# Expert weights applied at the copy out of PSUM, an accumulating scatter, and routing and first block reordered

## The chip, the cores and the metric

One NeuronCore of a Trainium2 chip runs the whole kernel. The metric is the device time of the execution in microseconds (us), as the median of the runs. The engines are PE (TensorE, matmul), DVE (VectorE), ACT (ScalarE), POOL (GpSimd) and SP (SyncE, which here only issues DMAs).

## The reference

One layer of a decoder trunk over 1024 prompt tokens and 32 sample tokens (TOK = 1056 rows of D = 1024, all float32). Attention, a recurrent branch and projections give x1; the change touches what follows:

```python
h2 = rms_norm(x1) * (1 + scale) + shift
g_logits = h2 @ w_rg + b_rg                    # 4 groups; g_star = argmax, p_group = softmax
in_group = (h2 @ w_re + b_re)[group g_star]    # 8 experts of the group
top_v, top_i = top_k(in_group, 2)
gate_w = softmax(top_v) * p_group[g_star]      # two weights per token
# the 2112 (token, expert) pairs, sorted by expert, in blocks of 128 rows of one expert
for each block: yb = (silu(x @ w_gate[e]) * (x @ w_up[e])) @ w_down[e]   # 1024 -> 512 -> 1024
moe[token] += yb * gate_w                      # two rows are added for each token
y = x1 + gate * rms_norm(moe)
```

There are 32 experts with 6.3 MB of weights each, and every expert's weights are read for at least one block. With these inputs there are 34 blocks.

## The kernel before

Tokens lie in nine tiles of 128 rows (the last has 32), in three groups of three tiles. The last group's mix (output projection) steps `mix(last, q)`, q from 0 to 7, are followed by norms, transposes and router logits of its three tiles; meanwhile DVE runs `best` (top group, top two experts) for the six earlier tiles. When the last logits are kept, DVE makes the one-hot of all 18 (tile, choice) pairs (`oh`, and `ohs`, their sum), PE ranks the pairs within their experts by 54 small matmuls with triangular and full ones (`ubf`, semaphore rt_pe 1), DVE turns ranks into slots (block, row) and one-hots of them, PE multiplies these with token numbers (18 matmuls, rt_pe 2), and DVE writes `slot_to` (destination row in y_dram: token, plus a plane offset for the second choice) and `slot_from` (token). GpSimd then gathers rows of h2 by an indirect DMA into `xg`. Softmax weights stay in `wts`, by token.

Every float32 matrix goes through PE as the sum of a rounded part and a rest: ACT rounds (`wg_up`, `wu_up`, `wd_up`, `x_up`, `a_up`), DVE subtracts (`wg_low` and so on), and PE does three products (up times up, up times low, low times up). A block n in steady state has on PE: transposes of the next block's x (L2282), up products of n (24 matmuls of 512 columns), first half of the gate products of n + 1, transposes of act_h (L2314), second half of the gate products of n + 1, and down products of n in two halves of the columns (y_half, y_done). ACT has x_up of n + 1, wd_up, one half of wu_up, a_up, the other half, the sigmoid, wg_up of n + 2 in two halves, and the two copies of y out of PSUM into `ysb[s]` (L1268, L1270). DVE has the matching subtractions and act_h (L1846), which stands behind both halves of wd_low. Each engine's instructions run in the order in which they are written. SP loads the weights of a block in the order gate, up, down, each when its buffer (two per matrix) is free. POOL's order in the loop is: gather of n + 3 (copy of the indices, indirect DMA), then scatter of n into y_dram (copy of the indices, indirect DMA). ACT's copy into `ysb[s]` waits for the scatter of n - 2 alone, by a semaphore for each of the two buffers. y_dram holds two planes, one row for each (token, choice), and no row is written twice.

The tail, when all scatters have landed: SP loads for each tile both planes' rows (`fy[:, t, 0:2, :]`, 1 MB), ACT multiplies the first by its weight (L1288), DVE adds the second times its weight (L1876), ACT squares and sums (L1296) and takes the root (L1298), DVE does the reciprocal, scales (L1888) and adds x1 (L1893), SP stores the tile. DVE's `add_second` of tile t + 1 stands ahead of the reciprocal of tile t.

## Time and profile before

| | us |
|---|---|
| median of 3 runs (1862.25 to 1864.72) | 1863.24 |
| the profiled execution | 1863.41 |
| its span | 1861.3 |

| engine | busy us | share |
|---|---|---|
| PE | 1707.8 | 92% |
| DVE | 1269.3 | 68% |
| ACT | 1053.0 | 57% |
| POOL | 269.4 | 14% |

The span is cut by the profile into 40 slices of 46.5 us. Attention and the recurrent branch run to about 600 us, the branch projections and the mix to about 1120, the last norms and the routing to about 1165, the expert blocks to about 1811 and the tail to 1861. DMAs moved 416.60 MB, 224 GB/s on the mean, but about 370 GB/s all through the expert blocks; 392.71 MB of them went on SP's queue and 17.73 MB on GpSimd's. A weight matrix of 2 MB lands 8 to 14 us after its issue there. The page's DMA line (busy tenths by slice) has 4 to 8 in the first six slices, 1 in the next seven, about 6 where the projections begin, and 8 to 9 in the expert blocks. The chain of the page has PE for 25% of the span, DMAs for 6%, DVE for 5%.

### The profile page before, as it was taken

The numbers are of one execution on the slowest core, as the hardware profiler recorded it, in microseconds if no ns is written. First come the engines' busy times: TensorE is split into PE (matmuls) and PEld (weight loads), VectorE is DVE, ScalarE is ACT, GpSimd is POOL, SyncE is SP. The second block draws the span as 40 slices with busy tenths as digits, with TensorE's granted clock in tenths as the row PEclk, the third lists the DMA queues.
The fourth block names the chain that finished last, engine by engine and source line by source line (L and its number), as shares of the span: only waits on it lengthen the run. The fifth ranks groups of instructions, "written<-read, shape, count | busy, mean of one in ns | idle before, by whom it ended". The sixth has DMA issues, their size and how long they took to land. (4 is left out here: it accounts for less than half of the span.)

```text
span 1861.3 us, 26670 instructions
## 1 busy us (share of the span) xinstructions
PE 1707.8 (92%) x10120; PEld 1473.3 (79%) x10120; DVE 1269.3 (68%) x1647; ACT 1053.0 (57%) x1465; POOL 269.4 (14%) x302
## 2 busy tenths in 40 slices
PE   6999889999999899999999994799999999999980
PEld 3889658888888899999999973587887888887860
DVE  4524367888887644545454667698988889998957
ACT  4535245555666533435344533578787877777745
POOL 0000011111110000000000200133333333242310
PEclk9999899999999899999999995899999999999995
DMA  8554441111111663734474663699999998998957
GB/s 346 185 184 142 159 163 48 55 52 49 50 49 57 247 203 124 260 124 152 159 258 151 205 227 124 251 386 373 384 373 375 363 378 351 367 373 348 378 198 279
DMA packets 101298, 416.60 MB, mean 224 GB/s; under 512 B 16039, under 2 KB 43847, under 8 KB 87496
## 3 DMA queue, kind: packets, MB, share of 16 engines
q1 hardware_dynamic: 85488, 392.71, 56.4%
q0 software_dynamic: 10704, 17.73, 2.6%
q10 hardware_dynamic: 5016, 4.93, 0.8%
q8 instruction: 61, 1.00, 0.2%
q14 instruction: 29, 0.24, 0.0%
HBM read 384.06 MB, written 51.13 MB: 234 GB/s over the span
## 5 line engine op out<-in xcount | busy, mean ns | idle before, releaser
L1076 ACT ACTIVATE wup<-wraw 128x1024 fp32r<-128x1024 f32 x120 | 126.7, 1059 | 274.7 <-PE ps L1898 238.8
L1564 DVE TENSOR_TENSOR wlow<-wraw,wup 128x1024 fp32r<-128x1024 f32 x120 | 146.8, 1224 | 166.2 <-ACT wup L1076 165.9
L1705 DVE TENSOR_TENSOR wg_low<-wg,wg_up 128x2048 fp32r<-128x2048 f32 x68 | 152.9, 2289 | 38.1 <-ACT wg_up L1190 38.1
L1705 DVE TENSOR_TENSOR wu_low<-wu,wu_up 128x2048 fp32r<-128x2048 f32 x68 | 155.6, 2289 | 16.9 <-ACT wu_up L1196 16.1
L1705 DVE TENSOR_TENSOR wd_low<-wd,wd_up 128x2048 fp32r<-128x2048 f32 x68 | 152.7, 2288 | 14.9 <-ACT wd_up L1243 14.8
L1190 ACT ACTIVATE wg_up<-wg 128x2048 fp32r<-128x2048 f32 x68 | 126.7, 1909 | 38.8 <-DMA wg<-w_gate 37.4
L1196 ACT ACTIVATE wu_up<-wu 128x2048 fp32r<-128x2048 f32 x68 | 130.1, 1914 | 25.0 <-PE ps L1898 25.0
L1026 ACT ACTIVATE pp<-ps,ngm 128x256 f32<-128x256 f32 x128 | 59.5, 470 | 136.4 <-DVE skd L1449 120.7
L1898 PE MATMUL ps<-h_up,wup 128*128 128x384 f32 (+1 forms) x384 | 128.1, 333 | 8.1 <-ACT yl L1148 4.2
L1898 PE MATMUL ps<-h_up,wlow 128*128 128x384 f32 (+1 forms) x384 | 126.7, 330 | 0.0
L1898 PE MATMUL ps<-h_low,wup 128*128 128x384 f32 (+1 forms) x384 | 126.6, 330 | 0.0
L1243 ACT ACTIVATE wd_up<-wd 128x2048 fp32r<-128x2048 f32 x68 | 126.3, 1911 | 0.0
L1898 PE MATMUL ps<-wg_up,x_up 128*128 128x512 f32 x272 | 112.2, 413 | 4.5 <-DVE x_low L1827 4.5
L1898 PE MATMUL ps<-wu_up,x_up 128*128 128x512 f32 x272 | 110.6, 407 | 0.0
L1898 PE MATMUL ps<-wd_up,a_up 128*128 128x512 f32 x272 | 108.7, 400 | 1.4 <-DVE a_low L1850 1.4
L1898 PE MATMUL ps<-hp_up,wA_up 128*128 128x352 f32 x312 | 108.2, 347 | 0.7 <-DVE hp_low L1327 0.7
L1898 PE MATMUL ps<-wg_low,x_up 128*128 128x512 f32 x272 | 108.1, 398 | 0.0
L1898 PE MATMUL ps<-hp_up,wB_up 128*128 128x352 f32 x312 | 106.4, 341 | 1.6 <-ACT gB L1001 1.6
L1898 PE MATMUL ps<-wg_up,x_low 128*128 128x512 f32 x272 | 107.8, 396 | 0.0
L1898 PE MATMUL ps<-wd_low,a_up 128*128 128x512 f32 x272 | 107.6, 396 | 0.0
L1898 PE MATMUL ps<-wd_up,a_low 128*128 128x512 f32 x272 | 106.8, 393 | 0.0
L1898 PE MATMUL ps<-wu_low,x_up 128*128 128x512 f32 x272 | 106.8, 393 | 0.0
(366 smaller groups left out, 4660.8 us busy)
## 6 DMA issues: line engine op xcount, KB each, us to landing
wg<-w_gate SPq DMA_DIRECT2D x34, 2048.0 KB, 12.6
wu<-w_up SPq DMA_DIRECT2D x34, 2048.0 KB, 13.5
wd<-w_down SPq DMA_DIRECT2D x34, 2048.0 KB, 8.2
wraw<-w_ga SPq DMA_DIRECT2D x24, 512.0 KB, 3.6
wraw<-w_gr SPq DMA_DIRECT2D x24, 512.0 KB, 3.6
wraw<-w_at SPq DMA_DIRECT2D x24, 512.0 KB, 3.5
wraw<-w_lr SPq DMA_DIRECT2D x24, 512.0 KB, 3.4
wraw<-w_out SPq DMA_DIRECT2D x24, 512.0 KB, 3.7
```

Of the source, the lines that this page charges most:

```text
L1026: act.activation(pp[:, s % 2, a, :], ps[:, 3 + s % 2, a * 2 * P:(a + 1) * 2 * P], ACT.Exp, bias=ngm[:, s % 2, a:a + 1], scale=SCALE, accum ...
L1076: act.activation(wup[n % UP][:, :, :], wraw[n % RAW][:, :, :], ACT.Copy).then_inc(w_rounded, 1)
L1190: act.activation(halves_of(wg_up)[h], halves_of(wg[s])[h], ACT.Copy).then_inc(g_rounded, 1)
L1196: act.activation(halves_of(wu_up)[h], halves_of(wu[s])[h], ACT.Copy).then_inc(u_rounded, 1)
L1243: act.activation(halves_of(wd_up)[h], halves_of(wd[s])[h], ACT.Copy).then_inc(d_rounded, 1)
L1564: V.tensor_tensor(wlow[n % RAW][:, :, :], wraw[n % RAW][:, :, :], wup[n % UP][:, :, :].bitcast(F32), ALU.subtract).then_inc(w_split, 1)
L1705: V.tensor_tensor(low[:, k0:k1, :], whole[:, k0:k1, :], up[:, k0:k1, :].bitcast(F32), ALU.subtract).then_inc(done, 1)
L1898: return pe.matmul(out, lhsT, rhs, start=start, stop=stop, skip_group_check=True)
```

## The change

1. Weights. After `wts`, DVE splits the weights into three bf16 parts (`wpart`) and multiplies the slots' block one-hot by them (`rhs3`); PE sends them to their slots by 18 matmuls of 144 columns (rt_pe 3), DVE adds the three parts into `wsl` (weight by slot and block). POOL copies a block's column into `wcur[:, s]` (`slot_weight`), and ACT's two copies out of PSUM take it as their scale, behind a wait on w_ready.
2. Scatter. y_dram has one row per token. SP writes zeros into it during the attention (nine DMAs). The scatter adds to the rows (`compute_op=ALU.add`) with the indices `slot_row`. POOL waits for each scatter's landing before it goes on; `st_y` is now one semaphore, and ACT's copy into `ysb[s]` waits for `32 * i`: all scatters of the pairs of blocks before its own.
3. Tail. One row per token is loaded (0.5 MB per tile), `weigh` and `add_second` are gone, the table for the root is loaded ahead of the first tile, and the addition of x1 goes to POOL for odd tiles.
4. Routing. `choose` makes the one-hots, for tiles 0 to 5 at q = 4 and for 6 to 8 at the end; PE's `rank` of tiles 0 to 5 goes behind the mix, the rest behind the last one-hot. PE's transposes of the last group wait for their own tile, with other banks. The last group's `best` is one tile and then two, and the second half of the first wg_low goes between them.
5. First block (`begin`). x_up/x_low of block 1 goes between the halves of its gate split, the subtractions wd_low of block 0 go behind act_h and a_low, and both halves of wu_up behind a_up.
6. Last block. The down weights of the last block are rounded into a buffer of their own (`wd_last`, in the gate buffer's place) already in the block before.

```diff
@@ -633,6 +641,12 @@
...
+                if i == 2:
+                    for t in range(TILES):
+                        n = P if t < BLKS else 2 * NS + 1
+                        sp.dma_start(y_dram[t * P:t * P + n, :].rearrange("p (a n) -> p a n", a=D // KV),
+                                     vtok[0:n, 0:1, :].broadcast_to([n, D // KV, KV])).then_inc(st_zero, 16)
+            sp.wait_ge(st_zero, 16 * TILES)
...
-                pool.tensor_copy(idx[:, 2 + s:3 + s], slot_to[:, bass.ds(n, 1)]).then_inc(idx_ready, 1)
+                pool.tensor_copy(idx[:, 2 + s:3 + s], slot_row[:, bass.ds(n, 1)]).then_inc(idx_ready, 1)
...
-                                        bounds_check=SPARE[1], oob_is_err=False).then_inc(st_y[s], 16)
+                                        bounds_check=TOK + NS, oob_is_err=False, compute_op=ALU.add).then_inc(st_y, 16)
+
+            def slot_weight(n, s):
+
+                pool.tensor_copy(wcur[:, s:s + 1], wsl[:, bass.ds(n, 1)]).then_inc(w_ready, 1)
...
@@ -845,14 +864,25 @@
...
+            pool.wait_ge(tables, 4)
+            for s in range(2):
+                pool.tensor_copy(wcur[:, s:s + 1], wsl[:, s:s + 1]).then_inc(w_ready, 1)
+            pool.wait_ge(st_zero, 16 * TILES)
...
                 for s in range(2):
...
+                    slot_weight(2 * i + s + 2, s)
+                    pool.wait_ge(st_y, 32 * i + 16 * s + 16)
             for s in range(2):
...
+                pool.wait_ge(st_y, 32 * more + 16 * s + 16)
...
+            pool.wait_ge(ld_x1, 32)
+            for t in range(1, TILES, 2):
+                pool.wait_ge(f_norm, t + 1)
+                pool.tensor_tensor(fy[:, t, :], fy[:, t, :], x1f[:, t, :], ALU.add).then_inc(y_added_p, 1)
...
         def _(act):
...
+            def act_block(i, s, ahead=2, begin=False):
...
+                if ahead >= 1 and not begin:
+                    round_x(n + 1, 1 - s)
                 if ahead >= 1:
-                    round_x(n + 1, 1 - s)
-                round_down(0, n, s, i + 1)
-                round_down(1, n, s, i + 1)
-                if ahead >= 1:
-                    round_up(0, n + 1, 1 - s, i + 1 + s)
+                    round_down(0, n, s, i + 1)
+                    round_down(1, n, s, i + 1)
+                    if not begin:
+                        round_up(0, n + 1, 1 - s, i + 1 + s)
...
+                if begin:
+                    round_up(0, 1, 1, 1)
                 if ahead >= 1:
...
@@ -1263,18 +1300,23 @@
                 if ahead >= 2:
...
+                if ahead == 1:
+                    round_last(0)
+                    round_last(1)
...
-                ge(act, st_y[s], 16 * i)
-                act.activation(ysb[:, s, 0:512], ps[:, 4, :], ACT.Copy)
+                ge(act, st_y, 32 * i)
+                act.wait_ge(w_ready, n + 1)
+                act.activation(ysb[:, s, 0:512], ps[:, 4, :], ACT.Copy, scale=wcur[:, s:s + 1])
...
-                act.activation(ysb[:, s, 512:1024], ps[:, 5, :], ACT.Copy).then_inc(y_kept, 1)
+                act.activation(ysb[:, s, 512:1024], ps[:, 5, :], ACT.Copy, scale=wcur[:, s:s + 1]).then_inc(y_kept, 1)
...
+            round_x(1, 1)
...
-            for s in range(2):
-                act_block(0, s)
+            act_block(0, 0, 2, True)
+            act_block(0, 1)
...
                 for s in range(2):
...
@@ -1282,18 +1324,11 @@
...
-            def weigh(t):
+            act.activation(fst[:, 0, 1:2], eps[:, :], ACT.Sqrt)
...
                 for t in range(t0, t1):
...
+            def choose(t0, t1):
+
+                ts, n = slice(t0, t1), t1 - t0
+                k(V.tensor_copy(eix[:, ts, :], ei8[:, ts, 0:2]))
+                k(V.scalar_tensor_tensor(eix[:, ts, :], bc(gix[:, ts].unsqueeze(2), (P, n, 2)), float(EPG), eix[:, ts, :], ALU.mult, ALU.add))
+                k(V.tensor_tensor(oh[:, ts, :, :].rearrange("p t k e -> p (t k) e"), bc(iot[:, 0:NE].unsqueeze(1), (P, 2 * n, NE)),
+                                  bc(eix[:, ts, :].rearrange("p t k -> p (t k)").unsqueeze(2), (P, 2 * n, NE)), ALU.is_equal))
+                V.tensor_tensor(ohs[:, ts, :], oh[:, ts, 0, :], oh[:, ts, 1, :], ALU.add).then_inc(rt_ready, 1)
+
             def split_half(h, whole, up, low, rounded, done, n):
...
@@ -1719,10 +1763,12 @@
...
                 if q == 4:
+                    choose(0, 3 * last)
+                if q == 4:
...
-                if q >= KC - 3:
-                    split_gate(q - KC + 3, 0, 0)
+                if q == KC - 3:
+                    split_gate(0, 0, 0)
...
             def last_half(j):
...
@@ -1754,19 +1800,16 @@
...
-            for j in range(2):
-                keep_logits(last, j, ((6, 1)[j], 0))
-            dve.wait_ge(lg_kept, 3 * last + 2)
-            best(3 * last, 3 * last + 2)
-            keep_logits(last, 2, (2, 0))
+            keep_logits(last, 0, (6, 0))
+            dve.wait_ge(lg_kept, 3 * last + 1)
+            best(3 * last, 3 * last + 1)
+            split_gate(1, 0, 0)
+            for j in (1, 2):
+                keep_logits(last, j, ((1, 2)[j - 1], 0))
...
-            best(TILES - 1, TILES)
-            k(V.tensor_copy(eix[:, :, :], ei8[:, :, 0:2]))
-            k(V.scalar_tensor_tensor(eix[:, :, :], bc(gix[:, :].unsqueeze(2), (P, TILES, 2)), float(EPG), eix[:, :, :], ALU.mult, ALU.add))
-            k(V.tensor_tensor(oh[:, :, :, :].rearrange("p t k e -> p (t k) e"), bc(iot[:, 0:NE].unsqueeze(1), (P, TK, NE)),
...
+            whole = wts[:, :, :].rearrange("p t k -> p (t k)")
+            k(V.tensor_copy(wpart[0][:, :], whole))
+            k(V.tensor_tensor(wrest[0][:, :], whole, wpart[0][:, :], ALU.subtract))
+            k(V.tensor_copy(wpart[1][:, :], wrest[0][:, :]))
+            k(V.tensor_tensor(wrest[1][:, :], wrest[0][:, :], wpart[1][:, :], ALU.subtract))
+            k(V.tensor_copy(wpart[2][:, :], wrest[1][:, :]))
+            for a in range(3):
+                ins = V.tensor_tensor(rhs3[:, :, a, :], ohblk[:, :, :], bc(wpart[a][:, :].unsqueeze(2), (P, TK, MAXB)), ALU.mult)
+            ins.then_inc(rt_ready, 1)
+            k(V.tensor_scalar(over[:, :], slot_to[:, :], 12, None, ALU.logical_shift_right))
+            k(V.scalar_tensor_tensor(slot_row[:, :], over[:, :], float(TOK), slot_from[:, 0:MAXB], ALU.mult, ALU.add))
...
-                if ahead >= 1:
+                if ahead >= 1 and not begin:
...
-                split_down(0, n, s)
-                split_down(1, n, s)
+                if ahead >= 1 and not begin:
+                    split_down(0, n, s)
+                    split_down(1, n, s)
...
-                if ahead >= 1:
+                if begin:
+                    split_down(0, 0, 0)
+                elif ahead >= 1:
...
+                if begin:
+                    split_down(1, 0, 0)
+                    split_up(0, 1, 1)
                 if ahead >= 1:
...
                 if ahead >= 2:
...
+                if ahead == 1:
+                    for h in range(2):
+                        split_half(h, wd[1], wd_last, wd_low[1], d_rounded, d_split, n + 1)
...
+            dve.wait_ge(rt_pe, 3)
+            k(V.tensor_copy(wsl[:, :], ps[:, 7, 0:MAXB]))
+            for a in (1, 2):
+                ins = k(V.tensor_tensor(wsl[:, :], wsl[:, :], ps[:, 7, a * MAXB:(a + 1) * MAXB], ALU.add))
+            dve.sem_inc(tables, 1)
...
+            split_x(1, 1)
...
-            with dve.Fori(0, more) as i:
+            dve_block(0, 0, 2, True)
+            dve_block(0, 1)
+            with dve.Fori(1, more) as i:
                 for s in range(2):
...
+
+            def rows(t):
+                return P if t < BLKS else NS
+
+            def rank(t0, t1):
+
+                for t in range(t0, t1):
+                    out = ps[:, 7, t * NE:(t + 1) * NE]
+                    for b in range(min(t + 1, TILES)):
+                        w = ubf[0:rows(b), 0 if b == t else 1, :]
+                        ins = mm(out, w, ohs[0:rows(b), b, :], b == 0, b == min(t, TILES - 1))
+                return ins
+
             for q in range(KC):
...
+            pe.wait_ge(rt_ready, 1)
+            rank(0, 3 * last)
...
-            pe.wait_ge(mix_kept, 6 * last + 6)
-            pe.wait_ge(mix_sq, 6 * last + 6)
             for j in range(3):
+                pe.wait_ge(mix_kept, 6 * last + 3 + j)
+                pe.wait_ge(mix_sq, 6 * last + 3 + j)
                 if j == 2:
...
-                turn(last, j, 0, (7, 4, 7)[j])
-                turn(last, j, 1, (3, 5, 3)[j])
+                turn(last, j, 0, (4, 0, 4)[j])
+                turn(last, j, 1, (5, 3, 5)[j])
+                if j:
+                    pe.wait_ge(mix_kept, 6 * last + 4 + j)
+                    pe.wait_ge(mix_sq, 6 * last + 4 + j)
...
-            pe.wait_ge(rt_ready, 1)
-
-            def rows(t):
-                return P if t < BLKS else NS
-
-            for t in range(TILES + 1):
-                out = ps[:, 7, t * NE:(t + 1) * NE]
-                for b in range(min(t + 1, TILES)):
-                    w = ubf[0:rows(b), 0 if b == t else 1, :]
-                    ins = mm(out, w, ohs[0:rows(b), b, :], b == 0, b == min(t, TILES - 1))
-            ins.then_inc(rt_pe, 1)
-
-            pe.wait_ge(rt_ready, 3)
+            pe.wait_ge(rt_ready, 2)
+
+            rank(3 * last, TILES + 1).then_inc(rt_pe, 1)
+
+            pe.wait_ge(rt_ready, 4)
             for q in range(TK):
...
+                down = wd_last if last else wd_up
                 for nn, done in enumerate((y_half, y_done)):
...
                     for m in range(FC):
                         if nn == 0 and m % 2 == 0:
...
-                        for a, w in ((a_up, wd_up), (a_up, wd_low[s]), (a_low, wd_up)):
-                            ins = mm(ps[:, 4 + nn, :], a[:, m, :], w[:, m, cols], m == 0 and a is a_up and w is wd_up, m == FC - 1 and a is a_low)
+                        for a, w in ((a_up, down), (a_up, wd_low[s]), (a_low, down)):
+                            ins = mm(ps[:, 4 + nn, :], a[:, m, :], w[:, m, cols], m == 0 and a is a_up and w is down, m == FC - 1 and a is a_low)
...
+            pe.wait_ge(rt_ready, 5)
+            for q in range(TK):
+                n = rows(q // 2)
+                ins = mm(ps[:, 7, 0:3 * MAXB], ohslot[0:n, q, :], rhs3[0:n, q, :, :].rearrange("p a b -> p (a b)"), q == 0, q == TK - 1)
+            ins.then_inc(rt_pe, 1)
...
```

## Rows read from the trace of the kernel before

**Rows 1.** busy us of PE, PEld, DVE, ACT, POOL; clock, DMA share, GB/s

```profile
1196.00:1500.00 304.00, 299.33 (x1381) 244.65 (x1380) 268.75 (x165) 233.84 (x181) 96.26 (x64) 1.00 0.90 365
```

**Rows 2.** the chain that ended last: start us, us, what

```profile
1223.65 0.89 PE ps L2282 x8
...
1537.62 0.89 PE ps L2282 x8
...
1555.66 0.89 PE ps L2282 x8
...
1811.86 3.15 DMA y_dram<-ysb,idx
```

**Rows 3.** waits in the expert blocks: who, for whom, us in total, times, longest

```profile
ACT wg_up L1190 <- DMA wg<-w_gate: 33.5, 26, 4.0
```

**Rows 4.** timeline of DVE, the tail's end: start us, us, engine, line, what

```profile
1851.28 1.23 DVE L1893 TENSOR_TENSOR fy<-fy,x1f 128x1024 f32<-128x1024 f32 x1
1852.43 1.27 DVE L1876 SCALAR_TENSOR_TENSOR fy<-fy,wts 32x1024 f32<-32x1024 f32 x1
...
1855.12 1.22 DVE L1893 TENSOR_TENSOR fy<-fy,x1f 128x1024 f32<-128x1024 f32 x1
...
1857.75 1.21 DVE L1893 TENSOR_TENSOR fy<-fy,x1f 32x1024 f32<-32x1024 f32 x1
```

**Rows 5.** timeline of ACT, the tail

```profile
1820.28 1.15 ACT L1288 ACTIVATE fy<-fy,wts 128x1024 f32<-128x1024 f32 x1 [9.63 <-DMA fy<-y_dram]
...
1830.64 1.06 ACT L1296 ACTIVATE fjunk<-fy 128x1024 bf16<-128x1024 f32 x1 [0.56 <-DVE fy L1876]
```

**Rows 6.** the tile qst: instructions, duration ns min/median/max, first and last start

```profile
L807 POOL COPY qst<-oT x128: 283/287/1238, 229.9 to 580.9; 64x128 f32<-64x128 f32 x128
```

**Rows 7.** timeline of POOL in the attention

```profile
459.00 2.51 POOL L807 COPY qst<-oT 64x128 f32<-64x128 f32 x2 [2.26 <-ACT oT L1055]
```

**Rows 8.** timeline of DVE at the same time

```profile
458.80 1.26 DVE L1512 SCALAR_TENSOR_TENSOR gC<-gC,yl 128x1056 f32<-128x1056 f32 x1 [3.25 <-ACT gC L1018]
460.10 1.26 DVE L1513 SCALAR_TENSOR_TENSOR olst<-gC,olst 128x1056 f32<-128x1056 f32 x1
```

**Rows 9.** the tensor y_dram, 1196 to 1793 us: its scatters' landings

```profile
DMA to landing us min/median/max: 5.2/11.1/12.0
```

**Rows 10.** the tile xg, 1196 to 1793 us: its gathers' landings

```profile
DMA to landing us min/median/max: 11.2/13.2/15.3
```

**Rows 11.** timeline of POOL: two of the scatters

```profile
1227.05 1.01 POOL L839 DMA_INDIRECT y_dram<-ysb,idx  x1 [0.90 <-POOL idx L836]
...
1778.12 1.03 POOL L839 DMA_INDIRECT y_dram<-ysb,idx  x1 [0.88 <-POOL idx L836]
```

**Rows 12.** timeline of ACT: the copies out of PSUM behind these

```profile
1241.92 0.58 ACT L1268 ACTIVATE ysb<-ps 128x512 f32<-128x512 f32 x1
...
1790.19 0.60 ACT L1268 ACTIVATE ysb<-ps 128x512 f32<-128x512 f32 x1 [2.26 <-PE ps L1898]
```

**Rows 13.** timeline of PE, last group and ranks

```profile
1126.87 1.94 PE L2203 MATMUL ps<-ident,xh 128*128 128x128 f32 x8 [7.40 <-DVE x L1730]
...
1146.52 1.95 PE L1898 MATMUL ps<-ohs,ubf 128*128 128x32 bf16 x54 [4.80 <-DVE ohs L1769]
```

**Rows 14.** the page's costliest groups: busy us, mean ns, idle before

```profile
L1705 DVE TENSOR_TENSOR wd_low<-wd,wd_up 128x2048 fp32r<-128x2048 f32 x68 | 152.7, 2288 | 14.9 <-ACT wd_up L1243 14.8
```

**Rows 15.** timeline of DVE, routing and first block

```profile
1158.83 2.03 DVE L1802 TENSOR_TENSOR rhs<-ohblk,tpid 128x864 bf16<-128x864 bf16 x2
...
1172.98 1.23 DVE L1827 TENSOR_TENSOR x_low<-ps,x_up 128x1024 fp32r<-128x1024 f32 x1 [1.05 <-ACT x_up L1238]
...
1194.26 0.68 DVE L1846 TENSOR_TENSOR act_h<-sgm,ps 128x512 f32<-128x512 f32 x1
```

**Rows 16.** timeline of the last block (PE's last up product, DVE)

```profile
1798.00 0.40 PE L1898 MATMUL ps<-wu_up,x_low 128*128 128x512 f32 x1
...
1799.73 0.68 DVE L1846 TENSOR_TENSOR act_h<-sgm,ps 128x512 f32<-128x512 f32 x1
```

More of the change, by code:

```diff
@@ L312, in build @@
         x1f = at("x1f", [P, TILES, D], ew0)
-        fy = at("fy", [P, TILES, 2, D], e0)
+        fy = at("fy", [P, TILES, D], e0)
+        wd_last = at("wd_last", [P, FC, D], e0, F32R)
         fjunk = at("fjunk", [P, D], ew0 + EW, BF16)
@@ L357, in build @@
         cmpb = rtm("cmpb", [P, MAXB - NE, NE])
+        rhs3 = rtm("rhs3", [P, TK, 3, MAXB], BF16)
+        wpart = [rtm(f"wpart{i}", [P, TK], BF16) for i in range(3)]
+        wrest = [rtm(f"wrest{i}", [P, TK]) for i in range(2)]
+        over = rtm("over", [P, MAXB], I32)
         iot = at("iot", [P, P], 3 * big - 2 * P)
@@ L367, in build @@
         mod_dram = nc.dram_tensor("mod_dram", [2, 4, AM, 512], F32)
-        y_dram = nc.dram_tensor("y_dram", [SPARE[1] + 1, D], F32)
+        y_dram = nc.dram_tensor("y_dram", [TOK + NS + 1, D], F32)
         def sem(name):
@@ L759, in _ @@
             sp.dma_start(x1f[0:NS, BLKS, :], x1_dram[SEQ:TOK, :]).then_inc(ld_x1, 16)
-            for s in range(2):
-                sp.wait_ge(st_y[s], 16 * more + 16)
-                sp.sem_inc(idx_seen, 1)
+            sp.wait_ge(st_y, 32 * more + 32)
+            sp.sem_inc(idx_seen, 1)
             for t in range(TILES):
@@ L1243, in round_down, with round_last @@
                 act.activation(halves_of(wd_up)[h], halves_of(wd[s])[h], ACT.Copy).then_inc(d_rounded, 1)
+            def round_last(h):
+                act.wait_ge(ld_d[1], 16 * more + 16)
+                act.activation(halves_of(wd_last)[h], halves_of(wd[1])[h], ACT.Copy).then_inc(d_rounded, 1)
             def gate_sigmoid(n):
@@ L1274, in _ @@
             round_gate(0, 1, 1, 1)
+            round_x(1, 1)
             round_gate(1, 1, 1, 1)
-            for s in range(2):
-                act_block(0, s)
+            act_block(0, 0, 2, True)
+            act_block(0, 1)
             with act.Fori(1, more) as i:
@@ L1282, in _ @@
             act_block(more, 1, 0)
-            def weigh(t):
+            act.activation(fst[:, 0, 1:2], eps[:, :], ACT.Sqrt)
+            for t in range(TILES):
                 n = P if t < BLKS else NS
                 act.wait_ge(ld_rows[t % LF], 16 * (t // LF + 2))
-                act.activation(fy[0:n, t, 0, :], fy[0:n, t, 0, :], ACT.Copy, scale=wts[0:n, t, 0:1]).then_inc(f_first, 1)
-            weigh(0)
-            for t in range(TILES):
-                n = P if t < BLKS else NS
-                if t + 1 < TILES:
-                    weigh(t + 1)
-                act.wait_ge(f_sum, t + 1)
-                act.activation(fjunk[0:n, :], fy[0:n, t, 0, :], ACT.Square, accum_out=fst[0:n, t, 0:1]).then_inc(ch_fin, 1)
+                act.activation(fjunk[0:n, :], fy[0:n, t, :], ACT.Square, accum_out=fst[0:n, t, 0:1]).then_inc(ch_fin, 1)
                 act.wait_ge(ch_fin, t + 1)
```

51 lines of the change are left out of this document (23 added, 28 removed).

## The prediction

> **What bounds the kernel now.** I read the page for the stages, then the busy time by stage, the chain of waits, the waits by pair, and the timelines of the three places that the diff touches.
>
> The expert blocks take a third of the span. From 1196 to 1500 us TensorE is busy 299.3 of 304 at a granted clock of 1.00 (2.4 GHz), VectorE 268.8, ScalarE 233.8, and the DMA engines 90% [rows 1]; the stretch on to 1793 is like it. The chain has PE's eight transposes at the head of a block 18.04 us apart [rows 2]: that is the pace, and there are 34 blocks. ScalarE waits for the gate weights in 26 of them, 33.5 us in total [rows 3], nearly all of it hidden behind PE's work. So three resources are within a tenth of each other here: the reader is to see that nothing may be added to the DMA queue or to ScalarE without asking twice. Behind the last block there is no PE work: VectorE repeats a cycle of 3.84 us per tile of the output, nine times, back to back [rows 4]. Ahead of the first block the routing is a serial chain on VectorE with PE and GpSimd taking turns. Tail and routing are pure latency, and what is taken out of them comes off the time in full.
>
> **The tail.** The last scatter lands at 1811.86 + 3.15 = 1815.0 [rows 2]; the span ends at 1861.3, so the tail is 46.3 us. The cycle [rows 4]: addition of x1 1.15 (1851.28 to 1852.43), then 2.69 for the addition of the second expert's row, the reciprocal and the scaling by norm and gain. The change takes out ScalarE's weighting (1.15 [rows 5]) and VectorE's second-row addition (1.27, of which 1.18 counts: instructions overlap by 0.09, as 1.23 and 1.15 show), leaving 2.69 - 1.18 = 1.51, and with the addition of x1 2.66 for the five even tiles; the four odd ones have 1.51, whose addition goes to GpSimd: 5 x 2.66 + 4 x 1.51 = 19.3. In front: the first tile came 5.2 after the landing with 1 MB [rows 5]; with 0.5 MB it is between 2.6 and 5.2, I take 3.9; square and root about 1.5 (1.06 for the square [rows 5], accumulator read and root behind it). The root's table is loaded early, under the load's latency. Behind: from the last addition's end at 1858.96 to the end 2.3 [rows 4]. Sum without GpSimd: 3.9 + 1.5 + 19.3 + 2.3 = 27.0, a gain of 19.3.
>
> GpSimd's additions are the unknown. Two copies of 0.28 each [rows 6] took 2.51 together when they met two VectorE instructions with two SBUF inputs; they ended when the second of those ended, and VectorE's lasted its plain 1.26 [rows 7, 8]. So GpSimd gave way to both, and did not get in between them. An addition of 1024 elements on GpSimd isn't in the trace: below, as on VectorE, 1.2; above, eight such copies for each of two inputs, 4.5; I take 2.3, eight copies. VectorE's reciprocal, one column with nothing read beside it, leaves a gap ahead of each scaling in which GpSimd can begin. If VectorE then waits, four additions cost 9.2, else nothing, for then they run beside it. I take the waiting: the tail is 36.2, gain 10.1, ends 19.3 and 1.3 (four at 4.5).
> The Trainium skill has this as a rule that speaks against the change (SBUF — State Buffer, "Who interferes with whom"): a VectorE instruction with two SBUF inputs contends with a GpSimd instruction that reads SBUF, as an exclusive lock held for a whole instruction. The trace shows the half in which GpSimd waits; by the rule VectorE waits too when GpSimd comes first, by the trace alone that stays open.
>
> **Accumulating scatter.** Its bytes: 2112 rows over 34 blocks, 62 rows of 4 KB, 0.25 MB more to read per block. At 365 GB/s [rows 1] that is 0.7 us of DMA per block in 18.04, a share of 0.90 becoming 0.94. Still under PE; but gate weights that land late already make ScalarE wait, so a few more blocks will slip: I take 3 us over the phase, from 0 to 15. The last scatter, alone on the queues, is on the path: with a read before the write between 0 and another 3.15, I take 1.5.
> New waits: GpSimd now waits for each scatter's landing before the next gather, which is queued behind it. Scatters land 11.1 after issue [rows 9], gathers 13.2 [rows 10]. A scatter is issued 3.4 after the head of the block (1223.65 to 1227.05 [rows 2, 11]), the next gather some 2.5 behind it; now it goes behind the landing: 3.4 + 11.1 + 2.5 + 13.2 = 30.2 into a block, needed two blocks on, at 36.1. Slack 5.9. Each even block's copy of its first half out of PSUM waits for the scatter issued in the same block (before, for the one ahead of it). Issue to copy, in the first of the 16 even blocks behind block 0: 1227.05 to 1241.92, 14.9; in the last: 1778.12 to 1790.19, 12.1 [rows 11, 12]; mean of the 16, 14.1. At 11.1 the wait costs nothing; at 14 it catches only blocks that wait for PE's second half anyway. The scale in the copy and the extra small GpSimd copy are hidden in the same gaps: 0.
> The Trainium skill (Collectives: The Full Stack, "The bandwidth ceiling: the fold count and why AG ≠ RS ≠ AR") has an add in the DMA read two sources, with two descriptors per chunk on one ring, so twice the read traffic. No row here has such a DMA; by that rule the sum would go the way of rival A, below, instead of the forecast's.
>
> **Zeroing y_dram** adds nine DMAs, 4.3 MB, near 362 us behind the y weights on SP's queue, with the gate-matrix load queued behind them. The page's DMA line has one tenth in that slice: the price is 0, and up to 2 if that load comes late.
>
> **Routing.** PE's first transposes of the last group waited for the third tile's half [rows 13]; now they wait for their own tile, and half a weight split (2.29, the size of those in [rows 14]) goes out of VectorE's way: between 0.6 and 2.0 earlier, 1.3. Of 54 rank matmuls in 1.95 [rows 13], 21 go ahead: 0.75. The one-hot of three tiles instead of nine saves 0.5, but two tiles instead of one go through the choice at the end, less than half a microsecond of it lost. Together -2.4 (from 1 to 4).
> Behind that the weights' table is added ahead of the up-weight split on VectorE: five tiny operations of 0.2, three products of 1.02 as the two in [rows 15], two of 0.2: 4.5. The first x_low at 1172.98 had 1.05 of idle ahead of it, so it comes at 1172.98 - 2.4 + 4.5 - 1.05 = 1174.0, 1.1 later than before. The routing gain is spent, and 18 matmuls lie in PE's idle time.
>
> **First block.** act_h (1194.26 [rows 15]) stood behind both wd_low halves, 2 x 2.29 less overlap, 4.4 [rows 14]; now it doesn't: 1.1 - 4.4 = -3.3. But both halves must still be done. VectorE owes 4.4 at the head of the second block and makes up 18.04 - 18.04 x 0.88 = 2.1 in a block, so PE waits some 2.3 there. Net -1.0, from +1 to -4.5 (nothing paid back, and PE's clock up earlier because it idles less).
>
> **Last block.** act_h was at 1799.73, PE's products done by 1798.4 [rows 16]; with wd_last it waits for PE alone: -1.3, with a shorter cold stretch -1.5 (0 to -3). The rounding moves into ScalarE's and VectorE's idle time before 1790.
>
> **Sum**, against the profiled execution's own 1863.41 (span 1861.3; 0.2 over the median of three runs, 1863.24): -1.0 (routing and first block) + 3.0 + 1.5 - 1.5 - 10.1 = -8.1, so 1855.3, and about 1855 by the median.
>
> **Rivals.**
> A, slower: the scatter's landing. Alone on the queues it lands in 3.15 [rows 2], beside the weights in 11.1 [rows 9]: its rows wait for turns among theirs. If the 62 rows of 128 that carry data take a second turn, half of the landing comes on top, 16.5. Then even blocks stall by 16.5 - 14.1 = 2.4 on ScalarE, 16 times, 38 us; where the second half wasn't ready (about a third) it is absorbed: +26, 1881. The gather is then 0.4 from its limit; at a landing of 22 it would be over it too, +110 and more. It decides from a landing of about 15. For it: ScalarE's chain to PE is tight; against: a row's two reads may go as one turn, +2 to 3.
> B, better: GpSimd's additions cost VectorE nothing, and the tail gives 19.3: 1846. For it: VectorE's instructions beside GpSimd's copies were never longer [rows 8]. Against: GpSimd's were tiny.
> C, no change: the DMA share is the true bound of the blocks, the extra read costs half of its 0.7 on each of 33 blocks, +12 instead of +3: 1864. For: the waits of [rows 3]. Against: PE at 98% in [rows 1].
>
> **Numbers.** Forecast 0.40 (own range 1849 to 1861), A 0.24, B 0.23, C 0.13. What this measurement can tell from no change is about 0.2%, 3.7 us. Faster by more: forecast nearly whole and B, 0.61; within: C and the edge, 0.14; slower: A, 0.25. The range that leaves 2 in 10 out: from 1842 (B with the better ends) to 1880 (most of A).
>
> **What would show it.** The landing of the y_dram scatters beside the weights (11 to 14 right, over 15 A); ScalarE's idle time before the first ysb copy in even blocks; turn-to-turn time 18.04 between 1200 and 1790; DMA share up by 0.04; VectorE's gaps in the tail equal to GpSimd's additions (lock) or none (B); x_low within 1.5 of 1174; the tail 36 (27 for B). Wrong if blocks grow by over 0.3 us each, or if the tail gives less than 8.

## The result: 2.1% slower, and the profile after

The changed kernel takes 1902.59 us (median of four runs, 1899.35 to 1904.34), the kernel before 1862.74 beside it: ratio 1.0211, 95% interval 1.0193 to 1.0229. Forecast were 1855 and a range up to 1880. The profiled execution is 1901.59 us, its span 1899.7.

The busy time by stage, in the window of [rows 1] and the one behind it (busy us of PE, PEld, DVE, ACT, POOL; clock, DMA share, GB/s):

```profile
1196.00:1500.00 304.00, 284.35 (x1267) 229.88 (x1266) 254.05 (x154) 218.03 (x169) 76.28 (x73) 0.97 0.89 341
1500.00:1830.00 330.00, 312.57 (x1415) 253.64 (x1414) 276.80 (x168) 241.35 (x185) 90.79 (x85) 0.98 0.85 332
```

In the first of them TensorE, VectorE and ScalarE do 5 to 7% less than in [rows 1], and GB/s falls from 365 to 341: nothing has become busier, all wait for something. TensorE's granted clock falls too, from 1.00 to 0.97; that is taken up below. The waits in the blocks (who, line, for what: us in total, times, longest) say for what:

```profile
POOL idx L841 <- DMA y_dram<-ysb,idx: 402.9, 31, 15.0
...
DVE x_low L1881 <- ACT x_up L1268: 48.4, 30, 3.3
ACT ysb L1309 <- DMA y_dram<-ysb,idx: 47.6, 15, 3.8
...
ACT wg_up L1220 <- DMA wg<-w_gate: 7.8, 14, 1.6
```

GpSimd (L841, the index copy ahead of the gather) spends 403 us waiting for landings, and ScalarE's even-block copy (L1309) is stalled 15 times. The wait for gate weights of [rows 3], 33.5 us, has shrunk to 7.8: weights are early now, because the rest is late. The landings beside the weights (first line the scatters, median 11.1 in [rows 9], second the gathers, median 13.2 in [rows 10]):

```profile
DMA to landing us min/median/max: 12.9/16.1/17.5
...
DMA to landing us min/median/max: 10.2/11.0/12.6
```

The chain of waits, which in [rows 2] ran along PE's transposes 18.04 us apart, runs from scatter to scatter, about 20 us apart, until the tail:

```profile
1327.67 16.02 DMA y_dram<-ysb,idx
1347.08 16.30 DMA y_dram<-ysb,idx
1367.15 15.94 DMA y_dram<-ysb,idx
1387.56 16.52 DMA y_dram<-ysb,idx
...
1855.89 5.71 DMA y_dram<-ysb,idx
1861.69 3.41 DMA fy<-y_dram
```

The next timeline, of GpSimd, ScalarE and VectorE in an even block, shows what hangs on a landing (start, us, engine, line, what, in brackets the idle time ahead and its releaser):

```profile
1347.08 2.74 POOL L854 DMA_INDIRECT y_dram<-ysb,idx  x1 [0.88 <-POOL idx L851]
...
1363.41 0.69 ACT L1309 ACTIVATE ysb<-ps,wcur 128x512 f32<-128x512 f32 x1 [3.51 <-DMA y_dram<-ysb,idx]
1363.96 0.18 POOL L841 COPY idx<-slot_from 128x1 int32 x1 [13.36 <-DMA y_dram<-ysb,idx]
...
1364.57 1.03 ACT L1268 ACTIVATE x_up<-ps 128x1024 fp32r<-128x1024 f32 x1
1365.00 1.05 POOL L844 DMA_INDIRECT xg<-h_dram,idx  x1 [0.86 <-ACT ysb L1311]
1365.63 1.23 DVE L1881 TENSOR_TENSOR x_low<-ps,x_up 128x1024 fp32r<-128x1024 f32 x1 [3.01 <-ACT x_up L1268]
1366.05 0.20 POOL L851 COPY idx<-slot_row 128x1 int32 x1
1367.15 1.59 POOL L854 DMA_INDIRECT y_dram<-ysb,idx  x1 [0.89 <-POOL idx L851]
```

One landing, at 1347.08 + 16.30 = 1363.4, releases two engines. GpSimd needs 3.8 us to the next scatter (0.6 to the copy, copy 0.2, 0.85, gather 1.05, copy 0.2, 0.89), so its loop is landing plus about 4. It waits for ScalarE's copies of y only twice in all the blocks: the loop, and not TensorE, sets when a scatter goes out. ScalarE has stood 3.51 us, its x_up and VectorE's x_low (3.01 idle) with it: TensorE is tied to the same landing.

What TensorE sees of it are pauses ahead of its transposes of act_h. The first line is the wait before the change, the second after it; then one of the pauses, and the clock right behind it (the stretch from 1373 to 1374 us; the clock is the 0.50):

```profile
PE ps L2314 <- DVE act_h L1846: 9.5, 8, 2.1
```

```profile
PE ps L2385 <- DVE act_h L1901: 37.4, 17, 2.6
```

```profile
1372.58 1.13 PE L2385 MATMUL ps<-ident,act_h 128*128 128x128 f32 x4 [2.55 <-DVE act_h L1901]
```

```profile
1373.00:1374.00 1.00, 1.00 (x6) 0.90 (x5) 1.00 (x1) 0.26 (x1) 0.00 (x0) 0.50 0.99 385
```

Before the pause the granted clock is 1.00 (2.4 GHz), behind it 0.50 (1.2 GHz) for some 3 us, with matmuls of 512 columns 0.43 us apart instead of 0.23; the same happens in ten of the 16 even blocks between 1208 and 1808 us. Over these 600 us the clock is 0.97 on the mean where it was 1.00, which takes 17 us of full clock away. By TensorE's account the blocks' 43.9 us below are some 28 of waiting for act_h and some 15 of lower clock. How many of the 43.9 would be left at full clock isn't shown; as GpSimd's loop hardly ever waits for TensorE, the lower clock may cost little of its own.

Where the 38.4 us of span went: to the first scatter +0.1 (1208.1 to 1208.2); from the first to the last scatter 603.8 to 647.7, **+43.9**; last landing 3.15 to 5.71, +2.6; from there to the end 46.3 to 38.1, -8.2. The first-to-last figure is used below for every kernel, from the row that gives its scatters' first and last start.

### The profile page after: what moved, and what is told of

Same layout as the page of the kernel before. It is cut to its first block and busy times, and to the rows that moved or that the text cites. A ratio compares the mean times of both kernels' runs of the same rounds, so it can differ in the third digit from the quotient of the medians.

```text
span 1899.7 us, 26818 instructions
## 1 busy us (share of the span) xinstructions
PE 1726.9 (91%) x10138; PEld 1485.3 (78%) x10138; DVE 1271.0 (67%) x1651; ACT 1048.2 (55%) x1457; POOL 260.4 (14%) x340
## 5 line engine op out<-in xcount | busy, mean ns | idle before, releaser
L1749 DVE TENSOR_TENSOR wg_low<-wg,wg_up 128x2048 fp32r<-128x2048 f32 x68 | 152.9, 2288 | 20.3 <-ACT wg_up L1220 20.1
L1959 PE MATMUL ps<-wg_up,x_up 128*128 128x512 f32 x272 | 119.0, 438 | 4.8 <-DVE x_low L1881 4.6
L1959 PE MATMUL ps<-wg_low,x_up 128*128 128x512 f32 x272 | 113.9, 419 | 0.0
L1959 PE MATMUL ps<-wg_up,x_low 128*128 128x512 f32 x272 | 112.9, 415 | 0.0
L1959 PE MATMUL ps<-wu_up,x_low 128*128 128x512 f32 x272 | 106.4, 391 | 0.0
L1959 PE MATMUL ps<-wd_up,a_up 128*128 128x512 f32 x264 | 104.8, 397 | 0.0
```

Of the source, the lines that this page charges most:

```text
L1749: V.tensor_tensor(low[:, k0:k1, :], whole[:, k0:k1, :], up[:, k0:k1, :].bitcast(F32), ALU.subtract).then_inc(done, 1)
L1959: return pe.matmul(out, lhsT, rhs, start=start, stop=stop, skip_group_check=True)
```

## The experiments

Three things came together in the blocks: the **addition** in the transfer, **GpSimd's wait** for the landing (ahead of the next gather), and **ScalarE's stricter wait** in even blocks. The experiments fill the table of the three. The kernel before, run beside them, had medians of 1860.6 to 1864.2 us, so a difference between two experiments' medians can be off by some us; where it matters, the one by the ratios is given too. "Landing" is from here on the median of all 34 scatters. The first theory was that GpSimd's loop alone did it.

**1. Plain scatter, both waits.**

```diff
-  ..., oob_is_err=False, compute_op=ALU.add).then_inc(st_y, 16)
+  ..., oob_is_err=False).then_inc(st_y, 16)
```

> The changed kernel with a plain scatter in the place of the accumulating one; every wait stays. It leaves out the addition of a token's two experts: the row written later overwrites the other. Theory (GpSimd's own loop: landing plus 4.3 us for the two index copies and two issues, against TensorE's 18.04 us a block): the landing beside the weights goes from 16.0 back to 11-12 us, the loop needs 15.5-16.5 us, TensorE sets the pace again at 18.04 us a block, and of the 47.3 us nearly all come back, with about 2.5 us at the last landing: 1851 to 1857 us. Rival A (ScalarE's wait in the 16 even blocks is what costs): the same direction, but only the 26 us priced on record come back, 1875 to 1880. Rival (the wait itself costs, whatever the landing): 1890 or more.

1865.28 us, 1.0017 of before (1.0000 to 1.0033). Neither number was met: the landing is 14.7, not 11 to 12.

```profile
1318.86 15.25 DMA y_dram<-ysb,idx
1337.90 15.65 DMA y_dram<-ysb,idx
1357.30 15.11 DMA y_dram<-ysb,idx
```

These three land in 15.3 on the mean, where the same plain scatter landed in 11.1: it now goes out right behind its predecessor's landing and a gather. The loop of these rows is 19.2 us, again the landing plus 4, and still above 18.04; over all blocks (616.8 us from the first to the last scatter) it is 18.7. TensorE's waits for act_h are 22.4 us, 13 more than before the change, which is all that the blocks have grown by; its clock stays at 1.00 from 1208 to 1808 us.

**2. ScalarE's wait relaxed, all else as changed.** Two semaphores in the place of one, so that each ysb half waits for its own last scatter.

```diff
-  ge(act, st_y, 32 * i)
+  ge(act, st_y[s], 16 * i)
```

> The changed kernel with ScalarE's wait in the even blocks put back from the scatter of the block before to that of two blocks before; GpSimd keeps its own wait for every landing. Theory (GpSimd's loop sets the pace, ScalarE's wait only shows it): no change, 1898 to 1904 us. Rival A on record (the even blocks' ScalarE wait costs 26 us over 16 blocks): 1874 to 1883.

1866.16 us, 1.0029 (1.0010 to 1.0047): some 35 us back. The theory with its fixed landing falls: GpSimd's wait is still there, and yet the blocks take 615.2. The chain shows how:

```profile
1384.28 10.72 DMA y_dram<-ysb,idx
1403.56 9.48 DMA y_dram<-ysb,idx
1417.93 13.52 DMA y_dram<-ysb,idx
```

The landing is 12.9 instead of 16.0, and it varies from 6.8 to 16.5: it isn't a constant of the transfer. That without ScalarE's tie the scatters drift against the weights' transfers, and some meet them at a better moment, would fit; it isn't shown.

The loop itself is still there. GpSimd goes on from a landing without any other wait in 30 blocks, and its scatters are 18.6 us apart on the mean. Its own part of the loop has grown: between the first two of these rows from the landing at 1395.0 to the next scatter at 1403.56, 8.6 us, and 6.4 on the mean of the chain's 28. The copy of the indices and the issue of the gather take longer (first two lines, 0.2 and 1.05 in the changed kernel's timeline above), and TensorE now waits for gathered rows, which it never did in the changed kernel (third line):

```profile
1395.57 2.10 POOL L842 COPY idx<-slot_from 128x1 int32 x1 [6.62 <-DMA y_dram<-ysb,idx]
...
1398.53 2.23 POOL L845 DMA_INDIRECT xg<-h_dram,idx  x1 [0.86 <-POOL idx L842]
```

```profile
PE ps L2354 <- DMA xg<-h_dram,idx: 15.2, 9, 2.8
```

TensorE's waits for act_h are down to 6.0 us, and its clock is 1.00 again from 1208 to 1808 us. In TensorE's account, the clock's 15 us are among those that came back.

**3. GpSimd's wait moved** from behind the scatter to right ahead of the next one; ScalarE's relaxed.

```diff
   pool.wait_ge(idx_ready, count)
+  ge(pool, st_y[1 - s], landed)      # the scatter of the block before
   ...
-  pool.wait_ge(st_y, 32 * i + 16 * s + 16)
```

> The changed kernel with GpSimd's wait for a landing moved from right behind its scatter to right ahead of the next block's scatter, so that the gather and both index copies run while the addition is under way; ScalarE waits for the scatter of two blocks before. Theory: the loop is the landing of 16.1 us plus one issue of about 1.1 us, 17.2 to 17.5, just under 18.04, so TensorE sets the pace, with a few us lost where a landing comes late: 1855 to 1864 us. Rival (the accumulating packets slow the weights' transfers and this sets the pace): 1885 or more. Rival (the landing grows once gather and scatter share the queue): 1870 to 1885, with a landing above 17 us in the row.

1873.35 us, 1.0062 (1.0042 to 1.0083), 619.9 us of blocks: in the band of the third line, but that line wanted a landing above 17, and it is 12.7: another reason. ScalarE's wait for gate weights is what grew:

```profile
ACT wg_up L1223 <- DMA wg<-w_gate: 53.6, 27, 4.5
```

**4. Addition without any wait.** A row for each of a token's two experts (index slot_to in the place of slot_row), both planes filled with zeros. The last pass reads one plane, so that the kernel leaves out the second expert's share, here and in experiments 5, 6, 8 and 10; in 1 and 7 the row written later replaces the earlier one.

> The accumulating scatter without any wait between blocks: each of a token's two rows has a row of its own (two planes, both filled with zeros ahead), so no order is needed; the last pass reads the first plane alone, which leaves the second expert's share out of the output. Theory (serial loop, not the addition's cost): landing still near 16 us or above, yet the blocks run at 18.04 us: 1852 to 1860 us. Rival (the addition's packets take the queues from weights and gathers): 1875 or more, with larger waits of ScalarE for the weights than the 7.8 us of the changed kernel.

1877.17 us, 1.0082 (1.0054 to 1.0110), blocks 619.7. The rival's side: with no wait at all the addition costs.

```profile
ACT wg_up L1218 <- DMA wg<-w_gate: 54.7, 27, 4.1
```

**5. Neither addition nor wait.** As 4, without compute_op.

> The changed kernel with a plain scatter and no wait between blocks (each of a token's rows has a row of its own; the last pass reads the first plane alone, so the second expert's share is left out): against add_no_wait (622 us from block 1's turn transposes to the last scatter) only the addition is gone. Theory (the addition takes DMA time that this stretch hasn't got to spare): the stretch falls back to about 606 us, as before the change, and the kernel to 1850 to 1856 us. Rival (the 16 us of add_no_wait are not the addition's, but come from the weights' scale, the block order or the chip): 1864 or more.

1846.93 us, 0.9924 (0.9898 to 0.9951), 3 below the band, blocks 602.0; the wait for gate weights is 24.0 us. The addition alone is worth 17.7 us of blocks in the profiled pair, and 30 between the medians: the profiled execution of add_no_wait lies 7 us below its median, that of plain_no_wait 6 above.

**6. Addition and ScalarE's wait.** As 4, with `if s == 0: ge(act, st_y[1], 16 * i)` ahead of the copy.

> add_no_wait with ScalarE's stricter wait in the even blocks alone: the copy of an even block waits for the scatter of the block before. GpSimd waits for no landing. The second expert's share is left out of the output. Theory (lockstep: the 36 us need both waits, since only GpSimd's wait puts the scatter right at the end of its own landing; without it a scatter goes out as soon as its rows are copied and has 16 us until the next copy): 1868 to 1880 us, as add_no_wait. Rival (ScalarE's wait by itself costs, as rival A on record): 1890 or more.

1875.52 us, 1.0056 (1.0035 to 1.0078), blocks 620.0: ScalarE's wait by itself costs nothing.

**7. Plain, GpSimd's wait only.** As 2, without compute_op.

> Plain scatter, GpSimd's wait for each landing kept, ScalarE's even wait relaxed; rows written later overwrite, the addition is left out. Theory (without ScalarE's wait the blocks are free of the scatter's time): 606 to 610 us for the stretch, 1850 to 1858 us in all, against 1865 with ScalarE's wait. Rival (GpSimd's loop of landing plus 4 us still sets the pace): the same 1862 to 1867 as with it, with 19 us from scatter to scatter.

1847.22 us, 0.9925 (0.9898 to 0.9951), blocks 593.6, landing 12.6: 3 below the band, and with a plain scatter GpSimd's wait costs nothing either.

**8. Plain, ScalarE's wait only.** As 6, without compute_op.

> plain_no_wait with ScalarE's stricter wait in the even blocks alone, the last corner of the table of addition, GpSimd's wait and ScalarE's wait (the second expert's share is left out). Theory (one wait closes no loop; a landing of 11 us is over before the next copy): 1845 to 1853 us, as plain_no_wait. Rival (ScalarE's wait costs by itself without the addition): 1860 or more.

1848.84 us, 0.9943 (0.9926 to 0.9960), in the band, blocks 595.9.

The table, median us and ratio to the kernel before:

| waits | plain | adding |
|---|---|---|
| none | 1846.9 (0.9924) | 1877.2 (1.0082) |
| ScalarE's | 1848.8 (0.9943) | 1875.5 (1.0056) |
| GpSimd's | 1847.2 (0.9925) | 1866.2 (1.0029) |
| both | 1865.3 (1.0017) | 1902.6 (1.0211) |

Neither wait makes the kernel longer without the other; together they cost 18 us without the addition and, from GpSimd's alone, 36 with it (17 and 34 by the ratios). With the addition GpSimd's wait alone is even 11 us better than none, but that is a balance of two things: TensorE waits 15.2 us for gathers (experiment 2; never in experiment 4), and ScalarE's waits for gate weights fall from 54.7 us to 20.1. That the wait keeps gather and scatter out of the gate weights' way would fit; it wasn't tried by itself.

**9. Both waits, but GpSimd's work out of the loop.** Experiment 3 with ScalarE's strict wait.

> wait_at_scatter (1873 us) with ScalarE's stricter wait in the even blocks put back: both waits of the changed kernel, but GpSimd's stands right ahead of the next scatter, with the gather and the index copies out of its loop. Theory (a closed loop: GpSimd goes from landing to next scatter in 4.1 us of its own work, ScalarE's wait ties TensorE to it; take the 4.1 us out and two waits cost nothing, as one): two blocks need twice a landing of 12.7 to 13.5 us plus 1.1 and 3.5 us of issue and copies, 30 to 32 us against TensorE's 36.1: 1870 to 1878 us, as without ScalarE's wait. If the landing went to 16.2 us again, 37.0 us for two blocks: 1885 to 1892. Rival (the pair of waits costs its 30 us wherever GpSimd's stands): 1897 or more.

1875.4 us, 1.0086 (1.0063 to 1.0110), blocks 617.0, landing 12.8. The closed loop stands: same two waits, same addition, and 27 us less than the changed kernel, which ran beside it. Which half of the loop gave them isn't separated, as both shrank: GpSimd's 4 us are out of it, and the landing is 12.8 instead of 16.0; either alone would bring the sum under 18.04 (16.0 + 1.1, or 12.8 + 4).

> The changed kernel as it is, on the chip of this comparison: 1898 to 1906 us, a landing of 15.5 to 16.5 us, 19.5 to 20.5 us from scatter to scatter. If it were much lower here, the price of the two waits together would be one of a chip and not of the kernel.

1902.95 us, 1.0225 (1.0201 to 1.0248), landing 16.0.

**10. Every plain scatter twice**, the second into a tensor that nobody reads, so that the queues are held as long as by the addition.

```diff
+  pool.indirect_dma_start(y_copy[:, :], ..., ysb[:, s, :], None, ...).then_inc(st_y[s], 16)
```

> plain_no_wait with every scatter issued twice, the second time into a tensor that nobody reads (the second expert's share is left out of the output as there). A valid row of 4 KB took 0.16 us in its queue as a plain write and 0.33 us as an adding one, so the second write costs the queues what the addition does. Theory (the addition costs its time in the DMA queues, next to weights that fill them to 0.9): the stretch from the first to the last scatter rises from 602 us by about 18, to 615 to 623 us, the kernel to 1862 to 1872. Rival (it is the read and write of one place, or the longer landing, that costs): 602 to 606 us, 1847 to 1852.

1865.50 us, 1.0014 (0.9996 to 1.0032), 18.6 over plain_no_wait (17 by the ratios), in the theory's band; blocks 610.6 in the profiled execution, below it. ScalarE's waits for gate weights are 42.1 us, between the 24.0 of experiment 5 and the 54.7 of experiment 4. The queues' share of the 16 engines' span (packets, MB, share), first of the kernel before, then of add_no_wait, then of this one:

```profile
q0 software_dynamic: 10704, 17.73, 2.6%
```

```profile
q0 software_dynamic: 10704, 17.73, 3.8%
```

```profile
q0 software_dynamic: 15600, 26.39, 3.8%
```

The addition moves the same bytes in 1.2% more of the engines' time, and a second write that takes the same 3.8% costs 17 to 19 of the addition's 30 us. So time in the DMA queues beside weights can be more than half of its price. The second write is not a pure copy of it: it has packets and an issue on GpSimd (1.02 us) of its own. What the other 11 to 13 us are isn't settled.

**11. Last additions on VectorE.** Experiment 2 with all nine additions of x1 on VectorE.

> act_wait_relaxed (1866 us) with all nine last additions on VectorE and none on GpSimd. Theory (GpSimd's additions lock VectorE out for about 2.1 us each, so that a pair of tiles takes 6.14 us against 2 times 2.66): the pass after the last landing falls from 38 us by 3 to 5 us, the kernel to 1861 to 1864 us. Rival (the two engines share the work without a lock, the ScalarE pass sets its pace): no gain, or up to 3 us slower.

1862.27 us, 0.9988 (0.9972 to 1.0005): 3.9 less than experiment 2 by the medians, but 7.6 by the ratios, and the tail agrees with the second: 31.5 us from the last landing to the end, where experiment 2 has 38.3. That is more than the 3 to 5 expected. Half of it is VectorE, which goes through a tile in 2.65 us:

```profile
1838.86 1.23 DVE L1948 TENSOR_TENSOR fy<-fy,x1f 128x1024 f32<-128x1024 f32 x1
...
1841.51 1.22 DVE L1948 TENSOR_TENSOR fy<-fy,x1f 128x1024 f32<-128x1024 f32 x1
...
1844.16 1.23 DVE L1948 TENSOR_TENSOR fy<-fy,x1f 128x1024 f32<-128x1024 f32 x1
```

The other half is the last store: from VectorE's last addition to the end 2.4 us, against 5.6 in experiment 2.

**12. Two planes, no addition in transit.** Plain scatter into two planes, no waits, no zeros; weights still at the copy out of PSUM; VectorE adds the planes.

```diff
+  V.tensor_tensor(fy[0:n, t, 0, :], fy[0:n, t, 1, :], fy[0:n, t, 0, :], ALU.add).then_inc(f_sum, 1)
```

> The changed kernel with a plain scatter into two planes and no wait between blocks, no zeros written, and the two planes added on VectorE in the last pass; weights still at the copy out of PSUM, and the earlier routing and first block stay. Theory: blocks as in plain_no_wait (602 us from the first to the last scatter), but the last pass is bound by VectorE's three operations a tile again (3.84 us), less one ScalarE pass of 1 us at its head, about 45 us: 1855 to 1860 us, 4 to 8 us below the kernel before. Rival (the addition in transit is worth its price because the last pass is shorter): above 1863.

1852.61 us, 0.9946 (0.9926 to 0.9966): faster than both kernels, by 10 us and by 50, and 2 below the band. It keeps the earlier routing, the first block and the last block of the change, and gives up the half-size last pass: its tail is 43.2 us, so the addition in transit is worth 12 us there (31.5 in experiment 11), less than it costs in the blocks.

**13. GpSimd's wait as a timing aid**, added to experiment 12 and, as one line, to the kernel before.

> two_planes with GpSimd's wait for each scatter's landing ahead of the next gather, which this kernel doesn't need for its result. Theory (the wait sets when gather and scatter enter the queues, and that helps: 593.6 us against 602.0 in the pair without the addition): 6 to 9 us below two_planes, 1847 to 1852 us. Rival (those 8 us were one execution's scatter, since the medians of that pair were equal, 1847.2 and 1846.9): within 2 us of two_planes.

> The kernel before with one line added: GpSimd waits for each block's scatter to land before the next gather. Theory (the wait helps by its timing): 594 to 598 us from the first to the last scatter instead of 603.8, 1853 to 1858 us. Rival (one execution's scatter): 1860 to 1866 us. Rival (GpSimd's loop, landing plus 4 us, holds up the gathers): 1870 or more.

1856.08 us, 0.9949 (0.9929 to 0.9969), and 1861.22 us, 0.9991 (0.9975 to 1.0008): no gain that can be told from none. The 8 us by which plain_pool_wait's blocks were shorter than plain_no_wait's were one execution's; the blocks of the kernel before take 603.5 with the line and 603.8 without it. The first-to-last figure of the changed kernel was 647.7 and 650.7, and plain_no_wait and two_planes, alike in the blocks, had 602.0 and 598.3; differences of that size are not argued from.

## Why the prediction was wrong

**The step that failed** is "Accumulating scatter", in two sentences. "At 11.1 the wait costs nothing; at 14 it catches only blocks that wait for PE's second half anyway", and the "slack 5.9" of the gather. Each wait was priced alone, against its own deadline, with a landing taken from a kernel in which no wait tied the scatter to anything. The experiments agree that neither alone makes the kernel longer. What was never worked out is the loop that GpSimd's wait closes: landing, 4 us of its copies and issues, next scatter, while ScalarE's copy, x_up and x_low hang on the same landing. Its period is landing plus 4, and it decides from a landing of 14 (18.04 - 4), the upper end of the landings of 11.1 to 14 that the forecast called free. In the changed kernel it is 16.0, the scatters are 19.6 us apart on the mean (18.3 before), and the blocks take 43.9 us more where the forecast had 3. The rows of the page allowed the sum of the loop: GpSimd's issue of 1.01 and the 0.90 between an index copy and its issue stand in [rows 11].

**The landing's size** was the second error, and the loop alone would not have been enough: at 11.1 its period is 15. From 11.1 the landing went to 14.7 by the two waits alone, to 12.7 by the addition alone, to 16.0 by all. Only 1.6 of the 4.9 us is the addition in itself. Why the waits lengthen it stays open; that the transfers meet the weights' at another moment is argued, not shown.

**TensorE's clock** had no term for the blocks. Its pauses of some 2.5 us in even blocks were followed by half the clock for some 3 us each, which took 17 us of full clock in all.

**The addition in the queues** was put at 3 us over the blocks, from 0 to 15; it is 17.7 by the profiled pair and 30 by the medians. Rival C had the mechanism (12 us), and was given 0.13. The added time in the queues was forecast right, 0.04 of the blocks: 1.2% of the span is 3.6% of them. "Still under PE" was the mistake: in add_no_wait, at a share of 0.95 from 1210 to 1500 (0.93 before), ScalarE's waits for gate weights are 54.7 us, where they are 24.0 without the addition.

**Rival A** had the landing (16.5) and the place (ScalarE's even blocks), and 1881 against 1902.6. Its 26 us come from 16 stalls of 2.4; measured are 15 stalls of 3.2, and removing its wait gave some 35 us back. What it lacked: that it needs GpSimd's wait beside it, and the addition's own price under it.

**Rival B** is refuted, the lock of the forecast is right. The tail of the changed kernel, VectorE and GpSimd:

```profile
1870.97 3.47 DVE L1950 SCALAR_TENSOR_TENSOR fy<-fy,fst,G2p 128x1024 f32<-128x1024 f32 x1
1871.02 2.34 POOL L885 TENSOR_TENSOR fy<-fy,x1f 128x1024 f32<-128x1024 f32 x1 [13.56 <-DVE fy L1950]
...
1874.48 1.22 DVE L1954 TENSOR_TENSOR fy<-fy,x1f 128x1024 f32<-128x1024 f32 x1
...
1877.18 2.34 POOL L885 TENSOR_TENSOR fy<-fy,x1f 128x1024 f32<-128x1024 f32 x1 [3.81 <-DVE fy L1950]
1877.20 3.39 DVE L1950 SCALAR_TENSOR_TENSOR fy<-fy,fst,G2p 128x1024 f32<-128x1024 f32 x1
```

GpSimd's addition takes 2.34 (2.3 was taken), and the scaling that starts beside it 3.4 instead of 1.28: it stands still until GpSimd is done. Two tiles take 6.14 us, where VectorE alone takes 5.30 (experiment 11). The forecast's 28.5 us for VectorE's part are 27.4; first tile 3.5 for 3.9, square and root 1.6 for 1.5. The tail came to 38.1 and not 36.2 by the last store, 5.4 us to its landing where the kernel before had 2.3. The runs show what it goes with: from VectorE's last addition to the end it is 5.5 us or more where GpSimd adds x1 for the odd tiles (the changed kernel, experiments 1 to 10), and 2.3 to 2.4 where VectorE adds all (the kernel before, experiments 11 to 13). Why is open. The Trainium skill's rule of an exclusive lock that runs in both directions (SBUF — State Buffer, "Who interferes with whom") is borne out by these rows for VectorE and by [rows 7, 8] for GpSimd.

**Smaller steps.** First x_low 1174.46 for 1174.0; act_h 1192.14 for 1191.0; block 1's transposes at 1202.15 instead of 1205.47 before; the last landing 5.71, +2.6 for +1.5; zeroing nothing (TensorE's busy time from 0 to 420 us 385.5 and 386.4). The Trainium skill's count of an adding transfer (Collectives: The Full Stack, "The bandwidth ceiling: the fold count and why AG ≠ RS ≠ AR") pointed the right way, though it is stated for collectives: here the addition takes as much more of the queues' time as a second write of its rows does, 1.2% of the span in both.

## What to carry to other kernels

When a change makes an engine wait for its own transfer, add up the loop that this closes (transfer, the engine's own work, next issue) and compare it with the pace of the bottleneck, above all where a second engine is tied to the same event; a slack worked out for each wait alone isn't enough. If an ordering wait is needed, put it right ahead of the instruction that needs it, with the engine's other work before it: here 27 us. And an addition in a transfer isn't free where the queues are nine tenths full: 30 us over 34 blocks by the medians, for a last pass that it shortens by 8, or by 15 with the last additions on VectorE.

## What the runs showed of the hardware

- Estimated from the queues' shares (1.2% of 16 engines' span over 2112 rows), an indirect write of a valid 4 KB row takes its queue about 0.17 us, and the addition as much again. Alone on the queues a plain scatter of 128 rows lands in 3.15 us, an adding one in 5.7; its issue takes GpSimd 1.02 and 1.59 us.
- The landing of one and the same plain scatter beside 6 MB of weights a block is 11.1 or 14.7 us, by the waits around it; of an adding one from 6.8 to 16.5 us within one execution (act_wait_relaxed).
- Behind pauses of some 2.5 us TensorE's granted clock was 0.50 for some 3 us (changed kernel); in experiments 1 and 2 its mean stayed at 1.00 through the blocks.
